# Hybrid decoder step: the key/value ring of the sample stage cut from twelve slots to ten, one weight chunk sent at the stage's start

## The reference, cut to what matters

```python
def layer_c_sample(x, c, page_table, pool_cmp_k, pool_cmp_v, pool_sel_k, pool_sel_v, win_k, win_v, ...):
    q, kcr, vcr, ks, vs, kw, vw, gates, z, gate = nsa_inputs(x, c, pos, norm_w, ada_w, ada_b, w_in, b_gate)
    ...
    o = nsa_attend(q, pos, gates, kc, vc, c_end, overlap, fetch_sel, kw_all, vw_all, kw_pos)
    y = nsa_output(x, o.reshape(B, T, NSA_WIDTH), z, gate, w_out)

def nsa_output(x, o, z, gate, w_out):
    y = (o.reshape(B, T, NSA_WIDTH) * silu(z)).astype(x.dtype)
    return x + gate * jnp.einsum('bte,ed->btd', y, w_out)
```

## Time and profile before

| what | value |
| --- | --- |
| median of 3 runs | 1494.87 us (1494.53 to 1496.16) |
| the profiled execution's own time | 1497.59 us |
| its span, first to last instruction | 1495.9 us |
| TensorE matmul busy | 1278.4 us (85%) |
| VectorE, ScalarE, GpSimd busy | 466.8, 413.2, 157.2 us |
| mean granted TensorE clock | 0.908 |
| DMA traffic of the whole program | 233.79 MB |

### The profile page before, as it was taken

The page is one execution under the profiler, slowest core; times in us unless marked ns, Lnnn a source line. Parts: engine busy times, 40 slices in busy tenths (PEclk is TensorE's granted clock), DMA queues, the critical chain, the costliest instruction groups (busy, mean ns, idle before and its releaser), DMA issues. The chain is left out here.

```text
span 1495.9 us, 25349 instructions
## 1 busy us (share of the span) xinstructions
PE 1278.4 (85%) x9349; PEld 824.1 (55%) x9349; DVE 466.8 (31%) x1456; ACT 413.2 (28%) x1091; POOL 157.2 (11%) x289
## 2 busy tenths in 40 slices
PE   4799999966859899999998999999977767678694
PEld 2576756724647637477786555555543333344472
DVE  0342110015561131112103655555543322222213
ACT  2221111121210130001011655556653333334000
POOL 0000000010000000000001222222223222222000
PEclk9899999986869989999985999999998987878798
DMA  8414333350031211122005666666668888776201
GB/s 347 169 57 169 113 113 113 113 179 0 1 96 66 76 64 57 61 91 113 0 0 177 231 231 234 230 233 230 230 220 323 325 311 310 284 283 226 113 0 63
DMA packets 73206, 233.79 MB, mean 156 GB/s; under 512 B 9722, under 2 KB 14972, under 8 KB 67068
## 3 DMA queue, kind: packets, MB, share of 16 engines
q1 hardware_dynamic: 50300, 156.67, 29.3%
q0 software_dynamic: 22784, 75.51, 13.4%
HBM read 215.10 MB, written 17.05 MB: 155 GB/s over the span
## 5 line engine op out<-in xcount | busy, mean ns | idle before, releaser
L376 PE MATMUL ps<-arena,wring 128*128 128x288 f32 x1920 | 481.4, 411 | 18.4 <-DMA wring<-in_weights 14.2
L376 PEld LDWEIGHTS ps<-arena,wring 128*128 128x128 f32 x1920 | 366.5, 192 | 125.1 <-DMA wring<-in_weights 14.7
L1479 POOL DMA_DIRECT2D arena<-in_cmp_pages x128 | 70.1, 549 | 490.6 <-issue 278.7
L383 PE MATMUL ps<-wring,arena 128*128 128x512 f32 (+1 forms) x240 | 107.6, 607 | 7.1 <-ACT arena L1180 7.1
L2013 ACT ACTIVATE arena<-arena 128x512 f32<-128x512 f32 (+1 forms) x88 | 57.3, 654 | 152.3 <-DVE arena L2049 152.3
L1573 DVE CUSTOM_DVE_ANT_0 wring<-ps,wring 128x128 f32<-128x128 f32 (+3 forms) x128 | 57.7, 488 | 75.8 <-PE ps L1502 74.4
L383 PEld LDWEIGHTS ps<-wring,arena 128*128 128x128 f32 (+1 forms) x240 | 43.4, 184 | 67.3 <-issue 67.3
L1565 ACT ACTIVATE wring<-ps 128x128 f32<-128x128 f32 (+3 forms) x128 | 49.1, 436 | 90.7 <-PE ps L1525 90.7
L1551 ACT ACTIVATE wring<-wring 128x128 f32<-128x128 f32 (+3 forms) x128 | 70.7, 559 | 9.0 <-DVE wring L1573 8.9
L1977 PE MATMUL ps<-fixed,arena 128*128 128x128 f32 x288 | 54.9, 327 | 18.9 <-ACT arena L2013 18.8
L1638 PE MATMUL ps<-arena 128*32 128x256 f32 x1024 | 70.3, 392 | 0.0
(11 more groups left out here) (360 smaller groups left out, 1515.6 us busy)
## 6 DMA issues: line engine op xcount, KB each, us to landing
wring<-in_weights SPq DMA_DIRECT2D x29, 2048.0 KB, 8.2
arena<-in_cmp_pages POOLq DMA_DIRECT2D x128, 256.0 KB, 4.3
arena<-in_cmp_pages SPq DMA_DIRECT2D x128, 256.0 KB, 3.4
arena<-in_kv_pages SPq DMA_DIRECT2D x64, 256.0 KB, 9.0
arena<-in_kv_pages POOLq DMA_DIRECT2D x64, 256.0 KB, 7.4
wring<-in_kv_pages SPq DMA_DIRECT2D x64, 256.0 KB, 9.7
wring<-in_kv_pages POOLq DMA_DIRECT2D x64, 256.0 KB, 7.4
wring<-in_win_kv SPq DMA_DIRECT2D x4, 1024.0 KB, 15.4
```

What stands on the lines that cost most here:

```text
L376: last = pe.matmul(out[:, 0:HT], w[:, k, ct * P:ct * P + P], moving[k][:, half * HT:half * HT + HT], start=(k == 0), stop=(k == KT - 1))
L383: last = pe.matmul(main[0:m, :], moving[k][:, index * P:index * P + m], w[:, k, :], start=(k == 0), stop=(k == KT - 1))
L1479: eng.dma_start(cring[q % CR][:, 2 * half + j, :], v["cmp_pages"][bass.ds(ids[2 * d + j], 1)] .rearrange("o p c -> (o p) c")).then_inc(c_i ...
```

## The change

The ring has ten slots instead of twelve: the two halves of the middle third of `wring` are taken out of the list. Right behind the loads of request 0 SP waits for the end of the prompt's products and of the last selection, and issues chunk 28 into that third. The last stage's `send_weights` then issues chunk 29 alone. Nothing that is computed changes.

```diff
-        KS = 12
+        KS = 10
...
-        kv_slots = cring_slots + [vv_[:, 0:SLOT]] + [wring_[:, s * SLOT:(s + 1) * SLOT] for s in range(6)]
+        kv_slots = cring_slots + [vv_[:, 0:SLOT]] + [wring_[:, s * SLOT:(s + 1) * SLOT] for s in (0, 1, 4, 5)]
...
                     for pair in range(NG // 2):
                         load_kv(sp, 0, n, pair)
                     load_window(sp, n)
+                    if n == 0:
+                        sp.wait_ge(pe_a, PE3["pv", U - 1])
+                        sp.wait_ge(dve_c, DC_["sel", NB - 1])
+                        send_weights(sp, W_OUT_C + 1)
```

## The result

The changed kernel takes 1516.7 us (median of 4 runs, 1514.7 to 1519.01), the kernel before 1495.26 us in the same comparison: ratio 1.0144, with a 95% interval of 1.0125 to 1.0163. It is slower by 21.4 us. The forecast was +12.3 us; the direction was right, the size too small, and 1516.7 lies just outside the stated range of 1499 to 1516.

The account below looks back on a forecast made before the run. Each request was taken as bound by the bytes landing between pv(0) and the window's scores. Requests 1 to 6 +14.9, request 7 +5.4, last stage -8.0 gave +12.3 us: median 1507.2 us, 8-in-10 range 1499 to 1516.

Parts of the forecast that it names:

- The mechanism: Sample stage: pv(0), the first product with the values, frees slots; bytes landing before the window's scores set each request's time.
- The last stage: End of kernel: chunk 28 is already there, so TensorE starts at 1394.4 instead of 1402.39 us: -8.0 us.
- Request 7: Last request, nothing follows its window, so no cushion: two more groups ahead of the window cost +5.4 us.
- Request 0 and the weights' transfer: Request 0: window, delayed behind the last selection, still lands in time; early weights replace two groups' bytes: cost nothing.
- Requests 1 to 6: Loads up to each window's scores: windows land 2.05 to 3.75 us later per request, in sum +14.9 us.
- the lower bound: Requests 1 to 6 with the slowest engine left out: 16.4 - 6 x 1.35 = 8.3 us.
- Full price: Rival, all seven requests: no cushion, 5.4 us each; +29.8 us in total, median 1524.7 us; chance 0.08.
- Mean, not slowest engine: Rival, requests 1 to 6: window's landing moves only with the engines' mean, +8.3 us; total +5.7, 1500.6 us; chance 0.22.
- Hidden loads: Rival: delays of requests 1 to 6 vanish, only request 7 pays; -2.6 us or less, 1492.3 us; chance 0.07.

Follow-up runs that it names:

- The ring alone: Changed kernel without the early weight send (ten slots, both weight chunks sent in the last stage), timed against the kernel before: 1526.3 us, ratio 1.0207.
- eleven slots: Kernel before with eleven ring slots instead of twelve and no early weights: 1512.6 us, ratio 1.0122 to the kernel before.
- the hold: Kernel before, with POOL waiting for a request's window to land before issuing its halves of the next request's groups 0 to 2: 1480.3 us, ratio 0.9886.

## Why the prediction was wrong in size

*The mechanism* stood: the loop through pv(0), the loads and the window, in which two groups pass from behind the window to ahead of it. The ring alone, eleven slots and the hold bear it out. The size was wrong, in one term.

*The last stage* (-8.0 us): right; the chain lost 7.93 us, and the ring alone is 9.6 us slower.

*Request 7* (+5.4 us): right, 5.5 us. Two groups at 2.70 us, and no next request's loads behind the window.

*Request 0 and the weights' transfer* (0): right. SP issued the window at 1125.69 us and the weights at 1126.15, and TensorE ran through the scores of groups 5 to 8 from 1130.13 without a wait. The timelines of both engines:

```profile
1125.69 0.34 SPq L1929 DMA_DIRECT2D wring<-in_win_kv  x1
1126.15 1.45 SPq L323 DMA_DIRECT2D wring<-in_weights  x1
```

```profile
1130.13 3.90 PE L1956 MATMUL ps<-wring,arena 128*64 128x512 f32 x16
```

*Requests 1 to 6* (+14.9 us): here the sum failed; it was 25.4 us. Two steps of it were wrong.

1. "The start-up, when slots come free one by one, is the same in both kernels." The prediction says this of request 7 and its sum takes it for every request. It is not so. The stores stand after pair 1 in POOL's order. With twelve slots the first load that pv(0) frees is the second of pair 1, so the stores follow it at once. With ten it is the second of pair 0, and POOL must first get two more slots. The start of the loads thus moved 240 GB/s instead of 274. I had compared how fast slots come free and not what else was in the queue beside them. Moving the stores back gave 9.4 us by the medians; between the two profiled executions it gave 6.7 us in the stretches of these six requests. This is the larger part.
2. "After the change only SP's half of one group still stands behind the window." In the mean of the engines nothing did (share 0.01). I had taken 1.35 us per request, 8.1 in all, as still behind it, and added 1.1 us per request, 6.6 in all, for the slowest engine. That the two nearly cancelled was luck. In the mean of the engines, all the 16.4 us of work that had stood behind the windows passed ahead of them, so the cost is 16.4 where I had 14.9. That is 1.5 us of the error. The half group was issued behind the window but landed beside it: in the DMA view of the changed kernel from 1268.5 to 1274 us (KB, us from issue to landing) the window, issued at 1268.92, took 17.1 us, and SP's two pages of the next request, issued from 1272.68 on, 13.6, so all landed near 1286 to 1287.

```profile
arena<-in_win_kv SPq DMA_DIRECT2D x1, 1024.0 KB, 17.1
...
wring<-in_kv_pages SPq DMA_DIRECT2D x2, 256.0 KB, 13.6
```

6.7 + 16.4 is 23.1 of 25.4 us. The remaining 2.3 us I can't assign; the six stretches of the ring alone and of the changed kernel differ by 2.2. The shares give a check of the split that needs no second kernel (share times length, over the six stretches): the engines were busy ahead of the windows for 154.7 us before and 172.9 after, and idle for 12.0 and 19.3. With the stores moved back they are 171.3 and 14.2. So some 18 us are work that passed to the front and some 7 are idle time, of which the stores' place accounts for 5. What I called the lower bound, 8.3 us, rested on the same half group; without it the mean of the engines gives 16.4.

*The rivals.* Full price (+29.8) did not occur in the sum, though requests 1, 2 and 6 came near its 5.4 us each, with 4.4 to 5.7 us. "Mean, not slowest engine" is refuted in its number, since the half group is not behind the window even in the mean. "Hidden loads" is refuted: no slack was found in any request.

## What to carry to other kernels

In a loop of prefetches, ask for each transfer that the next step waits for how many bytes pass ahead of it, and at which times of the loop the engines stand empty, not how busy they are on average. A prefetch for later that runs beside the awaited load delays it: holding three such half groups back won 14.5 us, in part because they then filled the empty start of the next round. When a ring gets shorter, check not only the loads but everything that sits at a fixed place in the same issue order: here a store that used to be issued early in the slow start slid behind two more waits, and moving it back gave 9.4 us. And before giving up slots for 8 us elsewhere, look at the order: the same twelve slots with stores and early loads behind the awaited window gave 32.6 us.

## What the runs showed of the hardware

The two queues don't share the engines by bytes. In the DMA view of the kernel before, between 1254 and 1260 us, when both had work:

```profile
q0 software_dynamic: 452, 1.48, 64.4%
q1 hardware_dynamic: 460, 0.84, 38.5%
```

The columns are packets, MB and share. POOL's queue (q0) and SP's (q1) had nearly the same number of packets, 452 and 460, but POOL's carried 1.48 MB and SP's 0.84: for the same kind of page load POOL's packets were almost twice as large on average. POOL's queue had 64% of the engines' time. The Trainium skill, "DMA: Bandwidth & Descriptors", section "Queues, rings and completion order", says that the engines take turns between queues packet by packet. The counts of this case agree where both queues have work.

So the window, which only SP carries, stands in the queue that gets the smaller share, and POOL's early loads overtake it. The 14.5 us that holding POOL back won fit this, but no run swapped the two queues, so how much of the gain comes from the unequal shares is not shown.
